# Conformer depthwise convolution: from VectorE chains and diagonal matmuls to stacked taps in four column strips

## What is computed

```
def causal_depthwise_conv(x, w):        # w: 31 taps x 1024 channels
    k = w.shape[0]
    return lax.conv_general_dilated(x, w[:, None, :], window_strides=(1,), padding=[(k - 1, 0)],
        dimension_numbers=("NWC", "WIO", "NWC"), feature_group_count=x.shape[-1])

def conformer_conv_mixer(x, w_pw1, b_pw1, w_dw, b_dw, ln_g, ln_b, w_pw2, b_pw2):
    h = x @ w_pw1 + b_pw1
    a, gate = jnp.split(h, 2, axis=-1)
    h = a * jax.nn.sigmoid(gate)
    h = causal_depthwise_conv(h, w_dw) + b_dw
    hf = h.astype(F32)
    mean = jnp.mean(hf, axis=-1, keepdims=True)
    var = jnp.mean(jnp.square(hf - mean), axis=-1, keepdims=True)
    hf = (hf - mean) * lax.rsqrt(var + LN_EPS) * ln_g + ln_b
    h = jax.nn.silu(hf)
    return h @ w_pw2 + b_pw2
```

## Time and profile before

| | |
|---|---|
| runs, us | 2121.66, 2123.98, 2125.15 |
| profiled execution: its own time, us | 2125.28 |
| its span, us | 2123.5 |
| TensorE busy | 2003.0 us, 94% |
| VectorE busy | 1323.7 us, 62% |
| ScalarE busy | 972.6 us, 46% |
| GpSimd busy | 77.5 us, 4% |
| mean granted TensorE clock | 0.964 |

### The profile page before, as it was taken

How to read it: one execution, slowest core, us unless ns; L and a number is a source line. 1 busy time by engine, 2 the same in 40 slices (tenths; PEclk the granted TensorE clock), 3 DMA queues, 4 the chain that set the end, 5 groups by cost and what they waited for, 6 DMA issues and landing times.

```text
span 2123.5 us, 25647 instructions
## 1 busy us (share of the span) xinstructions
PE 2003.0 (94%) x10412; PEld 1697.8 (80%) x10412; DVE 1323.7 (62%) x1721; ACT 972.6 (46%) x1265; POOL 77.5 (4%) x109
## 2 busy tenths in 40 slices
PE   6999999999999999999997579999999999999998
PEld 5778888877888777788887468888888888778887
DVE  4755665754666674476568956566666566556654
ACT  5544444553444543454446054445354454345443
POOL 0300000120000000000000000000000000000000
PEclk9889999979999999999998799999999999999999
DMA  7504654511765554456544117554556556535561
GB/s 239 175 1 139 194 187 155 191 65 41 229 196 186 185 195 154 131 178 197 185 141 147 43 52 233 183 197 149 198 171 197 188 183 201 167 119 170 197 198 61
DMA packets 197149, 340.58 MB, mean 160 GB/s; under 512 B 6757, under 2 KB 128233, under 8 KB 197032
## 3 DMA queue, kind: packets, MB, share of 16 engines
q1 hardware_dynamic: 193024, 331.04, 47.8%
q10 hardware_dynamic: 4008, 7.90, 1.1%
HBM read 337.88 MB, written 1.05 MB: 160 GB/s over the span
## 4 chain that ended last, share of the span: by engine, by line
PE 84%; DVE 9%; ACT 5%; issue 2%; DMA 0%; POOL 0%; DVEq 0%; ACTq 0%
PE ps L474 18%; PE ps L476 18%; PE ps L475 18%; PE ps L582 13%; PE ps L580 7%; DVE arena L1707 3%; PE ps L579 2%; DVE w_lo L1326 2%; ACT w_hi L892 2%; PE ps L729 1%; PE ps L744 1%; ACT xT L932 1%; PE ps L737 1%; PE ps L736 1%; ACT arena L926 1%
## 5 line engine op out<-in xcount | busy, mean ns | idle before, releaser
L1326 DVE TENSOR_TENSOR w_lo<-w_raw,w_hi 128x2048 fp32r<-128x2048 f32 x316 | 723.0, 2293 | 282.8 <-ACT w_hi L892 282.3
L892 ACT ACTIVATE w_hi<-w_raw 128x2048 fp32r<-128x2048 f32 x316 | 600.8, 1913 | 133.3 <-PE ps L476 127.0
L474 PE MATMUL ps<-w_hi,u_h 128*128 128x512 f32 (+1 forms) x1056 | 419.3, 397 | 9.8 <-DVE u_l L1683 3.0
L582 PE MATMUL ps<-xT,w_hi 128*128 128x512 f32 x1176 | 419.3, 396 | 0.0
L476 PE MATMUL ps<-w_hi,u_l 128*128 128x512 f32 (+1 forms) x1056 | 413.9, 392 | 0.0
L475 PE MATMUL ps<-w_lo,u_h 128*128 128x512 f32 (+1 forms) x1056 | 413.7, 392 | 0.0
L580 PE MATMUL ps<-xT,w_lo 128*128 128x256 f32 x1344 | 347.8, 279 | 0.0
L474 PE MATMUL ps<-w_hi,xT 128*128 128x512 f32 (+2 forms) x800 | 289.1, 361 | 8.2 <-DVE w_lo L1326 5.1
L476 PE MATMUL ps<-w_hi,xT 128*128 128x512 f32 (+2 forms) x800 | 285.0, 356 | 0.0
L475 PE MATMUL ps<-w_lo,xT 128*128 128x512 f32 (+2 forms) x800 | 284.9, 356 | 0.0
L580 PEld LDWEIGHTS ps<-xT,w_lo 128*128 128x128 f32 x1344 | 253.6, 189 | 13.6
(11 more groups left out here) (192 smaller groups left out, 1901.8 us busy)
## 6 DMA issues: line engine op xcount, KB each, us to landing
w_raw<-mlp_w_dram SPq DMA_DIRECT2D x128, 1024.0 KB, 5.4
w_raw<-ret_w_in_dram SPq DMA_DIRECT2D x48, 1024.0 KB, 5.2
w_raw<-w_up_dram SPq DMA_DIRECT2D x32, 1024.0 KB, 5.5
w_raw<-w_down_dram SPq DMA_DIRECT2D x32, 1024.0 KB, 4.8
w_raw<-w_in_dram SPq DMA_DIRECT2D x16, 1024.0 KB, 7.1
w_raw<-ret_w_out_dram SPq DMA_DIRECT2D x16, 1024.0 KB, 4.9
w_raw<-cf_w_pw_dram SPq DMA_DIRECT2D x12, 1024.0 KB, 5.2
w_raw<-sc_w_in_dram SPq DMA_DIRECT2D x12, 1024.0 KB, 5.2
```

Of the source, the lines that this page charges most:

```text
L474: pe.matmul(dst, lh, rh, start=start, stop=False)
L582: ins = pe.matmul(ps[:, bank, :], w_hi[:, slot, wsl], both, start=False, stop=kc == KC - 1)
L892: act.activation(w_hi[:, slot, :], w_raw[:, slot, :], ACT.Copy).then_inc(hi_ready[slot], 1)
L1326: tt(w_lo[:, slot, :], w_raw[:, slot, :], w_hi[:, slot, :].bitcast(F32), ALU.subtract).then_inc(lo_ready[slot], 1)
```

## The change

All eight blocks are now convolved on TensorE. A matmul takes 32 channels, not 128: its 128 contraction rows are those 32 channels four times, once for each of four neighbouring taps, and its weights are four diagonals of 32x32, one under another. The four groups g of 32 channels of a block go into the output partitions 32g to 32g+31, that is into four column strips of the array. Eight sets r of four taps cover 32 taps (the last is zero), so a block takes 8 x 4 = 32 fp32 matmuls of 128 rows, 32 output columns and 256 moving columns; the section takes 256.

The moving operand needs each group of 32 channels four times, shifted by 0 to 3 tokens: for each pair of blocks, 16 copies of 32 partitions x 2 x 284 elements from `cz` to `z_even` or `z_odd`, six on ScalarE (`Z_ACT`) and ten on VectorE, in the place of `cdiag` and `convolve`. The weights `tap_w` are built in the MLP section ahead: GpSimd sorts the taps, VectorE makes 16 small copies across partitions behind `prepare(2)`, and GpSimd makes eight products of 128x1024, paced by that section's `feed_lo`. TensorE's queue mixes the convolutions with the `up` calls, and the transposes, statistics and normalisation are split in two halves. `uadd` and `ulow` of all MLP sections now share the places of `relu` and `usq`.

```
-CONV_VEC, CONV_PE = (0, 1, 2, 3, 4, 5), (6, 7)
+Z_LEN, TAP_SETS = 284, 8
+Z_ACT = ((0, 0), (1, 0), (2, 1), (3, 1), (0, 2), (1, 3))
+        z_even = sb("z_even", [P, 4, 2, Z_LEN])
-        uadd = region(4096, 2, 512)
-        ulow = region(5120, 2, 512)
+        uadd = relu
+        ulow = usq
@@ tensor, cf
+                def conv(c):
+                    if c == 0:
+                        pe.wait_ge(taps_ready, 1)
+                    if c >= 4:
+                        pe.wait_ge(conv_a.sem, conv_a.at(sec, c - 3))
+                    pe.wait_ge(z_act.sem, z_act.at(sec, c // 2 + 1))
+                    pe.wait_ge(z_vec.sem, z_vec.at(sec, c // 2 + 1))
+                    for r in range(TAP_SETS):
+                        for g in range(4):
+                            ins = pe.matmul(ps[32 * g:32 * g + 32, c % 4, 0:S], tap_w[:, g, c, r, :],
+                                            z_pair(c // 2)[:, g, c % 2, 4 * r:4 * r + S], start=r == 0, stop=r == TAP_SETS - 1)
+                    ins.then_inc(conv_e.sem, 1)
...
+                up(sec, 6, 2, lambda: turn_ups(...))
+                conv(0)
+                conv(1)
+                up(sec, 7, 3)
+                pe.wait_ge(glu_done.sem, glu_done.at(sec, 1))
+                up(sec, 4, 4)
+                conv(2)
+                conv(3)
+                up(sec, 5, 5)
+                pe.wait_ge(glu_done.sem, glu_done.at(sec, 2))
+                up(sec, 6, 6)
+                up(sec, 7, 7)
+                conv(4)
+                conv(5)
                 pe.wait_ge(glu_done.sem, glu_done.at(sec, 4))
...
+                for t in range(NT):
+                    for c in range(4):
+                        ins = back(c, t)
                 ins.then_inc(conv_T.sem, 1)
+                conv(6)
+                conv(7)
+                pe.wait_ge(conv_a.sem, conv_a.at(sec, KC))
+                for t in range(NT):
+                    for c in range(4, KC):
+                        ins = back(c, t)
+                    ins.then_inc(conv_T.sem, 1)
@@ scalar, cf
-                        ins = act.activation(cdiag(d), ident[:], ACT.Copy, scale=gain("wdw", d % CFK, CONV_PE[d // CFK]))
+                    if j in (1, 2):
+                        conv_out(2 * j - 2)
+                        conv_out(2 * j - 1)
+                    act.wait_ge(glu_done.sem, glu_done.at(sec, j + 1))
+                    if j >= 2:
+                        act.wait_ge(conv_e.sem, conv_e.at(sec, 2 * j - 2))
+                    for t, g in Z_ACT:
+                        ins = act.activation(z_pair(j)[32 * t:32 * t + 32, g, :, :], cz[32 * g:32 * g + 32, 2 * j:2 * j + 2, t:t + Z_LEN], ACT.Copy)
+                    ins.then_inc(z_act.sem, 1)
@@ gpsimd, mlp ahead of cf
+                step.link(pool.tensor_copy(tap_rows, gcol[:, :, w:w + 32].rearrange("p c (r t) -> p t c r", t=4)))
...
+                for i in range(8):
+                    g, n = i // 2, slice(i % 2 * half, (i % 2 + 1) * half)
+                    pool.wait_ge(feed_lo.sem, feed_lo.at(sec, i + 4))
+                    ins = pool.tensor_tensor(tap_w[...][:, n, :], tap_mask..., tap_col..., ALU.mult)
+                ins.then_inc(taps_ready, 1)
@@ vector, mlp ahead of cf
+                    vec.wait_ge(taps_sorted, 1)
+                    for t in range(4):
+                        for g in range(4):
+                            ins = vec.tensor_copy(tap_col[32 * t:32 * t + 32, g, :], tap_rows[32 * g:32 * g + 32, t, :, :]...)
+                    ins.then_inc(taps_in, 1)
@@ vector, cf
-                def convolve(c):
...
+                    if j >= 2:
+                        vec.wait_ge(conv_e.sem, conv_e.at(sec, 2 * j - 2))
+                    for t in range(4):
+                        for g in range(4):
+                            if (t, g) not in Z_ACT:
+                                ins = vec.tensor_copy(z_pair(j)[32 * t:32 * t + 32, g, :, :], cz[32 * g:32 * g + 32, 2 * j:2 * j + 2, t:t + Z_LEN])
+                    ins.then_inc(z_vec.sem, 1)
```

More of the change, by code:

```diff
@@ L1125, in cf, with conv_out @@
             def cf(prev, sec):
+                def conv_out(c):
+                    act.wait_ge(conv_e.sem, conv_e.at(sec, c + 1))
+                    act.activation(ccv[:, c, :], ps[:, c % 4, 0:S], ACT.Identity, bias=gain("bdw", 0, c)).then_inc(conv_a.sem, 1)
                 begin(prev, sec)
@@ L1269, in mlp @@
             def mlp(sec):
-                pass
+                if not before_cf(sec):
+                    return
+                w = ROWS["wdw"]
+                step.link(pool.tensor_copy(tap_rows, gcol[:, :, w:w + 32].rearrange("p c (r t) -> p t c r", t=4)))
+                pool.memset(tap_rows[:, 3, :, TAP_SETS - 1], 0.0).then_inc(taps_sorted, 1)
+                pool.tensor_tensor(tap_mask, ident[:, 0:32], ident[:, 32:64], ALU.add)
+                step.link(pool.tensor_tensor(tap_half, ident[:, 64:96], ident[:, 96:128], ALU.add))
+                step.link(pool.tensor_tensor(tap_mask, tap_mask, tap_half, ALU.add))
+                pool.wait_ge(taps_in, 1)
+                half = KC * TAP_SETS // 2
+                shape = [P, half, 32]
+                for i in range(8):
+                    g, n = i // 2, slice(i % 2 * half, (i % 2 + 1) * half)
+                    pool.wait_ge(feed_lo.sem, feed_lo.at(sec, i + 4))
+                    ins = pool.tensor_tensor(tap_w[:, g, :, :, :].rearrange("p c r m -> p (c r) m")[:, n, :], tap_mask.unsqueeze(1).to_broadcast(shape),
+                                             tap_col[:, g, n].unsqueeze(2).to_broadcast(shape), ALU.mult)
+                ins.then_inc(taps_ready, 1)
             def attn(sec):
@@ L1305, in cf @@
             def cf(sec):
-                pool.wait_ge(gn_var.sem, gn_var.at(sec, 1))
-                rsqrt(grs[:, 0:2], gvar[:, 0:2], mv[:, 0:2, 1], 2, 1.0, LN_EPS).then_inc(gn_rs.sem, 1)
+                for t in range(NT):
+                    pool.wait_ge(gn_var.sem, gn_var.at(sec, t + 1))
+                    rsqrt(grs[:, t:t + 1], gvar[:, t:t + 1], mv[:, t:t + 1, 1], 1, 1.0, LN_EPS).then_inc(gn_rs.sem, 1)
             step.link(pool.memset(mhalf[:], -0.5))
@@ L1691, in cf @@
                 vec.memset(cz[:, :, 0:CFK - 1], 0.0)
+                vec.memset(cz[:, :, CFK - 1 + S:], 0.0)
                 begin(prev, sec)
                 prepare(sec, 0)
-                def convolve(c):
[L1696 to L1716, removed]
                 def glu(j):
@@ L1728, in glu @@
                     vec.wait_ge(glu_done.sem, glu_done.at(sec, j + 1))
+                    if j >= 2:
[5 more added lines that the diff above has]
+                    ins.then_inc(z_vec.sem, 1)
                 prepare(sec, 1)
                 glu(0)
[L1732 to L1740, removed]
+                for n in range(2, 7):
+                    prepare(sec, n)
+                    if n in (3, 5):
+                        glu(n // 2)
                 prepare(sec, 7)
@@ L1743, in cf @@
                 prepare(sec, 8)
-                for c in CONV_VEC[2:]:
-                    convolve(c)
                 vec.wait_ge(conv_T.sem, conv_T.at(sec, 1))
                 for t in range(NT):
-                    for h in range(2):
-                        ins = vec.bn_stats(bns[:, 2 * t + h, :], ps[:, 4 + 2 * t + h, :])
-                step.link(ins)
+                    vec.bn_stats(bns[:, 2 * t, :], ps[:, 4 + 2 * t, :])
                 for t in range(NT):
[L1752 to L1755, removed]
+                    vec.wait_ge(conv_T.sem, conv_T.at(sec, t + 2))
+                    step.link(vec.bn_stats(bns[:, 2 * t + 1, :], ps[:, 5 + 2 * t, :]))
+                    vec.bn_aggr(mv[:, t, :], bns[:, 2 * t:2 * t + 2, :].rearrange("p a b -> p (a b)")).then_inc(gn_var.sem, 1)
+                for t in range(NT):
+                    vec.wait_ge(gn_rs.sem, gn_rs.at(sec, t + 1))
+                    stt(gshift[:, t:t + 1], mv[:, t:t + 1, 0], -1.0, grs[:, t:t + 1], ALU.mult, ALU.mult).then_inc(gn_shift.sem, 1)
                 for k in range(4):
```

83 lines of the change are left out of this document (38 added, 45 removed).

## The result

The changed kernel takes **2090.18 us** (2089.23 to 2091.79 in four runs), the kernel before 2124.57 beside it: a ratio of 0.984 with a 95% interval of [0.9824, 0.9858]. The profiled execution took 2091.79 us, its span 2089.7 us, at a mean granted clock of 0.971.

What follows compares the result with a forecast made beforehand. VectorE was taken to bound the section. TensorE's steps summed to 1211.2, then 5.4 us more to 1216.6 against 1227.27 before: a gain of 10.6 us, 2125.28 to 2114.7, given as 2114 us, range 2105 to 2174.

Steps and rivals of the forecast that it cites:

- the price of a strip matmul: TensorE's 256 convolution matmuls: 0.225 us a call, only two column strips overlapping; its chance was 0.55.
- four side by side: Rival for the convolution matmuls: all four strips stream at once, 0.11 us a call, 2085 us; chance 0.12.
- Copies: Ahead of conv(0): VectorE's ten shifted copies take 4.0 us, ScalarE's six 3.5 us; TensorE idles 3.1 us.
- Slow clock: TensorE behind the idle gap at conv(0): the clock falls, costing 1.5 us.
- Convolutions: TensorE's eight blocks of 32 calls at 0.225 us: 57.6 us.
- Five `up`: TensorE's `up` matmuls for tiles 3 to 7, 48 each at 0.12 us: 28.8 us.
- No wait between: Between conv and `up` on TensorE: tile 4's `up`, 5.8 us, covers glu(1) and its copies, also 5.8 us.
- Transposes: Eight transposes on TensorE at full clock, at the end of the convolutions: 1.0 us.
- Tail: After TensorE's convolutions: conv_out(7), eight transposes, then statistics and normalising for the second token half, 5.4 us.
- Edits costed at nothing: MLP copies on VectorE, GpSimd's products, memsets, shared places and weight ring: all hidden, adding no time.
- couples of starts: Sign that the forecast was right: 512 strip records in 58 us, starting in couples almost together.
- fours at a time: Sign that the forecast was wrong: strip matmul records start four at a time, all four strips overlapping.

Runs made afterwards that it cites:

- the run of eight calls: Changed kernel with the strip matmuls reordered so each column strip gets all eight of its calls of a block in a row: 2148.0 us in one run.

## Why the prediction was wrong

**The step that failed is the price of a strip matmul.** "Matmuls start in the order of the queue, and the queue holds both records of a call before the next strip's first ... Only two strips ever overlap, and a call costs one record, 0.216 us." From it I took 0.225 us, where 0.11 was measured: exactly the lower bound, and the rival "four side by side" (chance 0.12, 2085 us) was the case. A matmul that waits for its strip does not block those behind it in the queue; a strip takes in about four. The stall that I argued exists, but it sets in only at runs longer than that, and a call has two records. I had put this limit at one by argument, with no row for it, and gave it 0.55; a range from 2105 then left out a bound that I had worked out myself.

The Trainium skill (TensorE: Matmul & The Clock Gate, Part 3: Packing small matmuls) has matmuls in different column groups at the same time, 2.38 times as fast for three. By that the change was more likely than I gave it, and this case agrees in kind: four strips gave 3.9 times. The prediction also has from there that starts keep program order. Here the measurement differs and decides: in the run of eight calls the next strip's first record starts within 0.01 us of the thirteenth of the former strip, whose last three start after it. The Trainium skill's rule that a load of weights overlaps only across row groups or into the background buffer did no harm: every strip here uses all rows, and four loads come together without a loss.

The chain by my steps, up to the transposes of `out_steps`, which I put at 1216.6 and which began at 1191.29:

1. *Copies.* After, groups by form from 1095 to 1225 (busy us, mean ns | idle before):

```profile
L1779 DVE COPY z_even<-arena 32x568 f32<-32x568 f32 x20 | 9.0, 448 | 0.3
...
L1194 ACT ACTIVATE z_even<-arena 32x568 f32<-32x568 f32 x12 | 8.1, 677 | 1.3 <-DVE arena L1770 1.2
```

   0.45 us and 0.68 us each, against 0.48 and 0.68 predicted: right, and odd offsets spoil nothing. But they follow each other with little overlap, 0.46 us from start to start where I had 0.40, so ten take 4.60 us and TensorE idled 3.72 us, not 3.1. With tile 2's `up` ending 0.4 us later, 1.0 us worse.
2. *Slow clock* behind the gap: 2.9 us against 1.5. I had scaled it from a stretch of `up` matmuls. 1.4 us worse.
3. *Convolutions*: 4 x 7.11 = 28.4 us against 57.6. 29.2 us better; this is the error.
4. *Five `up`*: 29.1 us against 28.8. "No wait between" missed 0.8 us ahead of conv(2), 1.1 us worse in all. VectorE's timeline there:

```profile
1140.21 0.88 DVE L1770 SCALAR_TENSOR_TENSOR arena<-ps,gcol,arena 128x256 f32<-128x256 f32 x2 [11.07 <-ACT arena L1184]
1141.12 4.60 DVE L1779 COPY arena<-arena 32x568 f32<-32x568 f32 x10
```

   From the first sigmoid of this pair (1139.34) to conv(2) (1145.88) are 6.5 us, where I had 5.8, and tile 4's `up` covers 5.8. Most of the difference is again the copies, 4.60 us and not 4.0. VectorE had stood idle for 11.07 us ahead of this glu, so the price of conv(0) and conv(1) has no part in it.
5. *Transposes*: 1.0 us, as predicted.
6. *Tail*: from the end of conv(7) to 1191.29 are 5.7 us against 5.4.

1.0 + 1.4 - 29.2 + 1.1 + 0.3 = -25.4, and 1216.6 - 25.4 = 1191.2.

**Behind the section.** TensorE is 36.0 us earlier there, the span only 33.8 shorter. I counted nothing for slow clock at the product, or up to 1 us of gain; in fact 13 matmuls are slow after and 9 or 10 before, about 1 us lost. The other 1.2 us or so are lost later in the program, 0.9 of them by the end of the short convolution section, which the change doesn't touch. Stretches in which the clock rises later are a possible reason that was not tested; the cause stays open. The worked 2085 of the rival was short of 2090 by these and by steps 1, 2 and 4.

**Edits costed at nothing** held. VectorE's 16 copies in the MLP and the last of GpSimd's eight products, after:

```profile
934.93 3.18 DVE L1485 COPY arena<-arena 32x64 f32<-32x64 f32 x16
```

```profile
1028.32 1.92 POOL L1327 TENSOR_TENSOR arena<-arena 128x1024 f32<-128x1024 f32 x1 [9.12 <-DVE u_l L1465]
```

3.18 us, inside 2 to 3.4; no new wait of TensorE stands in the MLP. The products took 1.92 us each and not 4.4, and were ready near 1030, over 90 us ahead of conv(0).

**The signs of the list**: couples of starts were the wrong sign, fours at a time the right one ("four at a time (side by side)"); the slow clock through the convolutions did not come; nothing waits for the taps.

## What to carry to other kernels

Four fp32 matmuls of 256 columns with 32 output rows each cost as much as one when they go to the four column strips, as long as the queue changes strips at least every four records (two fp32 calls); other sizes and types were not run here. Where no row gives a price, an argument from the order of the queue isn't enough to leave a bound out of the range that independent operations could reach. Once a matmul is this cheap, order the queue so that other matmuls cover what prepares its operands: moving one `up` was worth 10 us here, of which 3 were slow clock behind the gap. Filling a gap for the clock's sake shortened the stage here only when the second gap, ahead of the product, was filled too, and it was too small to be measured in the launch.

## What the runs showed of the hardware

- Four strips of 128x32 fp32 matmuls of 256 columns run in step: 0.11 us a call, against 0.43 in one strip.
- A strip takes about four matmuls ahead of its finish (3.8 to 3.9 records in three arrangements) before the queue behind it stalls, with one or two strips active; the room is each strip's own.
- During the first pair of 128x32 convolutions the granted clock rose from 0.50 to a mean of 0.79 in the rest of the pair, and it was 1.00 through the second pair.
- Behind 2.57 us in which TensorE was idle came matmuls of 512 columns 0.43 us apart, where they are 0.23 apart at full clock; with the gap filled, they started at 0.23 at once.
- ScalarE's and VectorE's copies of 32x568 took 0.68 and 0.45 us; GpSimd's product of 128x1024 1.92 us, less than the 2.2 us of 512 elements in the earlier trace rows, a different access whose cost was not looked into.
